# Three closing projections and the products behind them by halves of tokens, with three more pairs of split weights

## What is computed

```python
def rms_norm(x, g):
    y = xf * lax.rsqrt(jnp.mean(xf * xf, axis=-1, keepdims=True) + RMS_EPS)
    return (y * g.astype(jnp.float32)).astype(x.dtype)
...
    x = x + rms_norm(m, mix_post_g[layer])        # m = attention @ w_o
    f = conv_glu_ffn(rms_norm(x, ffn_pre_g[layer]), ...)
    x = x + rms_norm(f, ffn_post_g[layer])        # then kv, q of layer 1, or w_in of block two
```

## Time and profile before

| what | value |
|---|---|
| median of 3 runs | 1725.2 us (1720.46 to 1725.62) |
| the profiled execution, own time | 1720.62 us |
| its span, first to last instruction | 1718.8 us |
| PE busy | 1626.2 us (95%) |
| DVE, ACT, POOL busy | 1026.1, 697.8, 283.5 us |
| mean granted clock of PE | 0.97 |

### The profile page before, as it was taken

The page is one execution under the profiler, slowest core; times in us unless marked ns, Lnnn a source line. Parts: engine busy times, 40 slices in busy tenths (PEclk is TensorE's granted clock), DMA queues, the critical chain, the costliest instruction groups (busy, mean ns, idle before and its releaser), DMA issues.

```text
span 1718.8 us, 20823 instructions
## 1 busy us (share of the span) xinstructions
PE 1626.2 (95%) x7828; PEld 1297.6 (75%) x7828; DVE 1026.1 (60%) x1824; ACT 697.8 (41%) x1349; POOL 283.5 (16%) x227
## 2 busy tenths in 40 slices
PE   6899999999898889999999989999998999999996
PEld 6678888888676668888888867866665788888875
DVE  4766666643767657666663267576666445554364
ACT  4344444332436635444442243244344343333252
POOL 2411111000402213111110035000010021110031
PEclk9899999999898989999999989999999999999998
DMA  4133333323121113333333224221110233333221
GB/s 143 37 99 97 95 98 98 104 93 101 56 68 32 38 55 92 98 97 95 97 99 98 92 62 123 68 56 38 38 44 19 86 86 98 98 98 97 95 92 61
DMA packets 89340, 139.24 MB, mean 81 GB/s; under 512 B 8596, under 2 KB 28564, under 8 KB 89240
## 3 DMA queue, kind: packets, MB, share of 16 engines
q1 hardware_dynamic: 86464, 133.56, 26.4%
q10 hardware_dynamic: 2776, 4.35, 0.8%
HBM read 135.78 MB, written 2.10 MB: 80 GB/s over the span
## 4 chain that ended last, share of the span: by engine, by line
PE 90%; DVE 6%; issue 1%; ACT 1%; POOL 1%; DMA 0%; SPq 0%; POOLq 0%; DVEq 0%; ACTq 0%
PE ps L347 24%; PE ps L349 24%; PE ps L348 24%; PE ps L1580 2%; PE ps L1582 2%; PE ps L1581 2%; PE ps L359 1%; PE ps L1263 1%; PE ps L1286 1%; PE ps L1306 1%; PE ps L381 1%; PE ps L645 1%; PE ps L960 1%; DVE M L485 0%; DVE M L468 0%
## 5 line engine op out<-in xcount | busy, mean ns | idle before, releaser
L335 DVE TENSOR_TENSOR wl<-raw,wh 128x512 fp32r<-128x512 f32 (+2 forms) x472 | 360.9, 767 | 491.8 <-ACT wh L324 491.6
L324 ACT ACTIVATE wh<-raw 128x512 fp32r<-128x512 f32 (+2 forms) x472 | 295.3, 627 | 665.5 <-PE ps L349 658.2
L347 PE MATMUL ps<-Hh,wh 128*128 128x512 f32 (+1 forms) x1336 | 531.9, 398 | 29.0 <-DVE Hl L408 21.0
L349 PE MATMUL ps<-Hh,wl 128*128 128x512 f32 (+1 forms) x1336 | 525.2, 393 | 0.0
L348 PE MATMUL ps<-Hl,wh 128*128 128x512 f32 (+1 forms) x1336 | 525.1, 393 | 0.0
L347 PEld LDWEIGHTS ps<-Hh,wh 128*128 128x128 f32 (+1 forms) x1336 | 253.6, 190 | 95.9 <-DVE Hl L408 28.1
L349 PEld LDWEIGHTS ps<-Hh,wl 128*128 128x128 f32 (+1 forms) x1336 | 253.4, 190 | 54.5 <-issue 0.2
L348 PEld LDWEIGHTS ps<-Hl,wh 128*128 128x128 f32 (+1 forms) x1336 | 253.9, 190 | 52.6 <-issue 0.9
L347 PE MATMUL ps<-AH,wh 128*128 128x512 f32 x480 | 187.1, 390 | 0.0
L349 PE MATMUL ps<-AH,wl 128*128 128x512 f32 x480 | 186.9, 389 | 0.0
L348 PE MATMUL ps<-AL,wh 128*128 128x512 f32 x480 | 186.8, 389 | 0.0
(11 more groups left out here) (254 smaller groups left out, 1653.5 us busy)
## 6 DMA issues: line engine op xcount, KB each, us to landing
raw<-in_w_in SPq DMA_DIRECT2D x216, 256.0 KB, 2.7
raw<-in_w_out SPq DMA_DIRECT2D x104, 256.0 KB, 2.6
raw<-in_w_up SPq DMA_DIRECT2D x64, 256.0 KB, 2.7
raw<-in_w_down SPq DMA_DIRECT2D x32, 256.0 KB, 2.8
raw<-in_w_q SPq DMA_DIRECT2D x16, 256.0 KB, 2.6
raw<-in_w_o SPq DMA_DIRECT2D x16, 256.0 KB, 2.6
raw<-in_w_pg SPq DMA_DIRECT2D x16, 256.0 KB, 2.8
X<-in_xT SPq DMA_DIRECT2D x8, 256.0 KB, 6.0
```

The costliest lines, as they stand in the source:

```text
L324: e.activation(spls[n % NSPL][0][:, 0:width], raws[n % NRAW][:, 0:width], ACT.Copy, scale=1.0 if gain is None else gain).then_inc(s_hi, 1)
L335: e.tensor_tensor(wl[:, 0:width], raw, wh[:, 0:width].bitcast(F32), ALU.subtract).then_inc(s_lo, 1)
L347: e.matmul(b, wh[:, o:o + w], xh, start=k == 0, stop=False)
L349: m = e.matmul(b, wl[:, o:o + w], xh, start=False, stop=k == nk - 1)
```

## The change

At the three boundaries the last three pieces of the closing projection are held back and multiplied for tokens 0 to 255 in all four tiles, then for tokens 256 to 511. The norm of each half is its own chain (`half_*` functions with two blocks of tokens), with a bank of PSUM for each half, and squares are no longer paired: PE sums each half tile by itself. The gain goes into the take, so that the scale is a plain multiplication. The first three right-hand tiles and products of the next stage are done by halves too; POOL now adds tiles 2 (two halves), 4, 5, 6, 7 and DVE 0, 1 (two halves) and 3. Pieces 1 to 3 of the next stage get pairs of their own (`more`, in the arena that the closing projection has partly finished with), so they can be split before the held pieces are free. Three small constants move to make room. `kv`, `in1` and `z` are the stages behind.

```diff
+        more = [(sub(f"xh{i}", [P, NPIECE], 24576 + 4096 * i, F32R), sub(f"xl{i}", [P, NPIECE], 26624 + 4096 * i, F32R))
+                for i in range(3)]
...
-            for n in range(start, start + nk - 1):
+            held = 3 if closing else 1
+            for n in range(start, start + nk - held):
...
-        ON_DVE = (0, 1, 5)
-        ON_POOL = (2, 3, 4, 6, 7)
+        X_ON_DVE = {1: [(0, 1), (1, 1), (5, 1)]}
+        X_ON_POOL = {1: [(2, 1), (3, 1), (4, 1), (6, 1), (7, 1)]}
+        for v in (2, 3, 4):
+            X_ON_DVE[v] = [(0, 0), (1, 0), (0, 1), (1, 1), (3, 1)]
+            X_ON_POOL[v] = [(2, 0), (2, 1), (4, 1), (5, 1), (6, 1), (7, 1)]
...
         def act_rhs(e, j, k):
+            if j in (1, 2, 3):
+                if k == 0:
+                    for half in range(2):
+                        for c in range(3):
+                            rhs_high(e, j, c, half)
+                    rhs_square(e, j, 0)
+                elif k < 6:
+                    rhs_high(e, j, k + 2)
+                    rhs_square(e, j, k)
+                else:
+                    rhs_square(e, j, k)
+                return
...
         def pe_first_group(e, j, name, nk, outs, free):
+            halved = 3 if j in (1, 2, 3) else 0
+            for half in range(2):
+                for k in range(halved):
+                    e.wait_ge(s_hl, rhs_at(f, k, half))
...
+                        m = multiply_half(e, b, wh[:, o:o + w], wl[:, o:o + w], Hh[:, k, :], Hl[:, k, :], half,
+                                          k == 0 and half == 0, False)
...
+                    if k == 0 and half == 0:
+                        half_spread(e, j, 1)
+            for k in range(halved, nk):
...
+        def pe_close(e, q, name, xh, xl, nk):
+            n = first[name] + 2 * nk - 3
+            for half in range(2):
+                for i in range(4):
+                    bank = Q_BANKS[q][i]
+                    if half:
+                        e.wait_ge(s_pev, tile_at(q, 4 + i, 0))
+                    for k in range(3):
+                        if half == 0 and i == 0:
+                            e.wait_ge(s_lo, n + k + 1)
+                        h, l = (x[:, i * P:(i + 1) * P] for x in split_in[n + k])
+                        m = multiply_half(e, bank, h, l, xh[:, nk - 3 + k, :], xl[:, nk - 3 + k, :], half, False, k == 2)
+                        if k == 2:
+                            m.then_inc(s_acc, 1)
+                        if k == 1 and half + i > 0:
+                            a, b = (half, i - 1) if i else (0, 3)
+                            e.wait_ge(s_psq, tile_at(q, 4 + b, a))
+                            half_square(e, q, a, T[POST_T[q][4 + b]], False, b == 3)
+                        if k == 1 and half and i == 3:
+                            half_spread(e, q, 0)
+            e.wait_ge(s_psq, tile_at(q, 7, 1))
+            half_square(e, q, 1, T[POST_T[q][7]], False, True)
+
+        def dve_close(e, q):
+            for i in range(4):
+                half_take(e, q, i, 0)
+            half_variance(e, q, 0)
+            half_take(e, q, 0, 1)
+            half_take(e, q, 1, 1)
+            half_diagonal(e, q, 0)
+            half_take(e, q, 2, 1)
...
         def dve_new_rhs(e, q, j, k):
+            if k == 0 and q > 0:
+                scale_m(e, q, 0, 0)
+                add_m_dve(e, q, 0, 0)
+                half_take(e, q, 3, 1)
+                half_variance(e, q, 1)
+                rhs_low(e, j, 0, 0)
+                scale_m(e, q, 1, 0)
+                add_m_dve(e, q, 1, 0)
+                half_diagonal(e, q, 1)
+                scale_m(e, q, 2, 0)
+                rhs_low(e, j, 1, 0)
+                scale_m(e, q, 0, 1)
+                add_m_dve(e, q, 0, 1)
+                rhs_low(e, j, 2, 0)
+                scale_m(e, q, 1, 1)
+                add_m_dve(e, q, 1, 1)
+                rhs_low(e, j, 0, 1)
+                scale_m(e, q, 2, 1)
+                rhs_low(e, j, 1, 1)
+                scale_m(e, q, 3)
+                add_m_dve(e, q, 3)
+                rhs_low(e, j, 2, 1)
+                scale_m(e, q, 4)
+            elif q > 0:
+                if k < 4:
+                    scale_m(e, q, k + 4)
+                if k < 6:
+                    rhs_low(e, j, k + 2)
```

More of the change, by code:

```diff
@@ L251, in build, with group @@
         n_acc = n_used = 0
-        def group(name, g, start, nk, tiles):
+        def group(name, g, start, nk, tiles, closing=False):
             nonlocal n_acc, n_used
             acc_base[name, g] = n_acc
-            for n in range(start, start + nk - 1):
+            held = 3 if closing else 1
+            for n in range(start, start + nk - held):
                 n_used += 1
                 used[n] = (s_used, n_used)
-            n_acc += tiles
-            used[start + nk - 1] = (s_acc, n_acc)
+            n_acc += tiles * (2 if closing else 1)
+            for n in range(start + nk - held, start + nk):
+                used[n] = (s_acc, n_acc)
         for n in (0, 2):
@@ L269, in build @@
             for g in range(2):
-                group("out" + name, g, first["out" + name] + NTILE[l] * g, NTILE[l], 4)
+                group("out" + name, g, first["out" + name] + NTILE[l] * g, NTILE[l], 4, l < 2 and g == 1)
             if l == 0:
@@ L384, in keep_root, with half_bank, half_square @@
         def keep_root(e, k, bank):
-            e.wait_ge(s_spread, k)
+            e.wait_ge(s_spread, CHAIN_AT[k] - 1)
             e.activation(RB[:, :], bank[:, :], ACT.Copy).then_inc(s_rb, 1)
+        def half_bank(q, half):
+            return Q_BANKS[q][POST_BANK + half]
+        def half_square(e, q, half, sq, begin, end):
+            bank, o = half_bank(q, half), 256 * half
+            for b in range(2):
+                m = e.matmul(bank[:, o + b:o + b + 1], sq[:, (2 * half + b) * P:(2 * half + b + 1) * P], mean[:, 0:1],
+                             start=begin and b == 0, stop=True, skip_group_check=True)
+            if end:
+                m.then_inc(s_stat, 1)
@@ new lines, in act_close, with half_take @@
+        def act_close(e, q, name):
+            for half in range(2):
+                for i in range(4):
+                    e.wait_ge(s_acc, acc_base[name, 1] + 4 * half + i + 1)
+                    if half == 0 and i == 0:
+                        e.wait_ge(s_pair, pairs_at(q) + 2)
+                    c = slice(256 * half, 256 * half + 256)
+                    e.activation(T[POST_T[q][4 + i]][:, c], Q_BANKS[q][i][:, c], ACT.Square).then_inc(s_psq, 1)
+        def half_take(e, q, i, half):
+            e.wait_ge(s_psq, tile_at(q, 4 + i, half))
+            c = slice(256 * half, 256 * half + 256)
+            e.tensor_scalar(M[:, 4 + i, c], Q_BANKS[q][i][:, c], col(POST_GAIN[q], 4 + i), None,
+                            ALU.mult).then_inc(s_pev, 1)
@@ L742, in pe_ffn @@
                 outs = [L_BANKS[l][4 * ((G + h) % 2) + i][:, :] for i in range(4)]
-                for k in range(nt):
+                closing = l < 2 and h == 1
+                for k in range(nt - 3 if closing else nt):
                     if h == 0:
@@ L811, in dve_ffn @@
                         dve_rotation(e, k)
+                if l < 2 and h == 1:
+                    dve_close(e, q + 1)
+                    continue
                 for i in range(4):
@@ L836, in gpsimd_ffn @@
             if l < 2:
-                root(e, POST_CHAIN[q])
+                for half in range(2 if q else 0):
+                    half_root(e, q, half)
+                if q == 0:
+                    root(e, POST_CHAIN[0])
                 add_m_pool(e, q)
```

270 lines of the change are left out of this document (176 added, 94 removed).

## The result

| | before | after |
|---|---|---|
| median of six runs | 1725.2 us | 1731.5 us |
| range of the runs | 1720.5 to 1726.6 | 1728.6 to 1733.5 |
| ratio, 95% interval | | 1.0043 [1.0027, 1.0059] |
| the profiled execution | 1720.6 us | 1733.5 us |

The change makes the kernel 6.3 us slower, where 8 were forecast. This is one comparison; further down the same kernel comes out 4.5 us apart in two of them, so the sign is firm and the size is not. The two profiled executions are 12.9 us apart, since before's is one of its fastest and after's is its slowest.

The account below looks back on a forecast made before the run. PE, busy 1626.2 of 1718.8 us, was taken as the bound, gated by POOL's sums. Boundaries of +2.1, +2.3 and +3.4 made about +8: span about 1727, 1733 against the 1725.2 median; range 1711 to 1740.

Parts of the forecast that it names:

- main case: At three boundaries PE waits for POOL's later sums and the clock falls: +8 us, 1733 against the median; chance 0.42.
- How well the gate was hidden: Behind product 6 PE needs POOL's six sums of squares, today hidden by only 0.9, 0.3 and 1.2 us.
- DVE's list: From first spread to last scale DVE needs 17.1 us instead of 11.8; POOL's last addition ends 19 us after that spread.
- short waits for the second spread and ACT, +1.3: Part of DVE's added time between the first spread and the end of its last scale: 1.3 us per boundary.
- rival (d): Low clock also catches the half products opening the new stage, at most one boundary: +5 us, 1738; chance 0.05.
- The six sums: POOL's six sums at 1.71 us each, 10.25 in all as today, ending at 461.7 instead of 460.4 at the first boundary.
- (b): POOL's six sums meet few collisions, 2.7 us less each boundary, and the clock stays up: 1716 us; chance 0.15.
- (c): POOL's sums are ready when PE asks, so product 7 starts 5.2 us sooner or more: 1707 us; chance 0.11.
- The low clock behind the gate: After 6.9 us of only mean squares, product 7 starts at 1.2 GHz: +2.0 us at the first boundary.
- Rival (a): Clock holds through the light stretch or sums end a microsecond sooner: about 1726 us; chance 0.27 shared with late halves.
- The third boundary: ACT's five transfers delay the first right-hand half, starting 2 us later than in the second stage: boundary +3.4 us.
- Rival (e): Halves wait for the whole root, starting behind the second spread near 437; same time as the clock holding, shared chance 0.27.

Follow-up runs that it names:

- e5_warm: Changed kernel plus four fp32 products of 512 columns, unused in the result, in PE's wait between the two mean squares: 1725.9 us, ratio 1.000 to before.
- moderate: Changed kernel with four POOL sums, scale 5, one split, then scales 6 and 7, constants' transfers later: 1714.7 and 1719.2 us, 0.994 and 0.9966 of before.
- with filler: The moderate kernel plus one unused fp32 product of 512 columns behind each closing's last half square: 1718.9 and 1718.3 us, 0.997 and 0.996 of before.
- all in full: Changed kernel with four POOL sums, scales 4 to 7 in a row ahead of the splits, constants' transfers later: 1728.4 and 1729.9 us, both 1.002 of before.

## Why the prediction was right, and where its terms were off

- **The main case held:** 1733 forecast, 1731.5 measured. The mechanism is the one forecast, a gate that was hidden and is not any more. Its three signs are all there: first products 5.2 us sooner at the first boundary (5.9 forecast), a new wait for the sums of 4.0 us three times (4 to 5), the clock at 0.50 when product 7 starts.
- **How well the gate was hidden was misread:** the prediction has PE ask for the sums at the start of its two mean squares (461.36). The last sum is needed by the second of them, some 0.8 us later, so the sums were hidden by 1.8, 1.2 and 2.0 us, not 0.9, 0.3 and 1.2. The forecast does not suffer, since it uses only the differences between the three, and in the new order it rightly does one mean square ahead of the wait.
- **DVE's list:** POOL's last addition was to end 19 us after the first spread; it ended 21.5, 20.4 and 23.4 after. The step was right, its size short by 1 to 4 us. The term that was mis-sized is "short waits for the second spread and ACT, +1.3": DVE idles 1.97 us for the second spread alone at the first boundary. In part it was made good by luck: the first spread came 12.3 and 11.6 us behind the start of the closing at the first two boundaries, where 12.9 were forecast.
- **The reason is rival (d), in part.** It was given 0.05 as a case of its own, since "PE's gaps there are under 1 us". They were 1.09 and 2.73 us, and the clock fell at the first and third boundary (in 436 to 440, and from 1017). Twelve half products then took 12 x 0.21 instead of 12 x 0.12, 1.1 us, and the second spread came that much later: 2.6 us behind the first new product, against 1.5 at the second boundary, where the clock fell only behind it (638.04). This accounts for most of the +4.0 instead of +2.1 at the first boundary, with +2.2 of it ahead of product 7; the second, which escaped it, gave +1.6, less than forecast. The kernel with filler products (e5_warm) allows a comparison here, since it is the same up to the first mean square and its clock held in this hole:

```profile
435.37 0.39 PE L412 MATMUL ps<-Hh,wh 128*128 128x256 f32 x1 [1.09 <-DVE Hl L514]
436.92 0.59 PE L482 MATMUL ps<-DG,ones 128*128 128x256 f32 x2
...
452.14 10.16 POOL L529 TENSOR_TENSOR M<-M 128x512 f32<-128x512 f32 x6
```

Both kernels reach the first new product 15.5 us behind the start of the closing (419.89 here). From there the second spread comes 1.6 us behind it, not 2.6, and the sums end 42.4 us behind the start of the closing, not 43.9. The forecast was 42.2. So this fall costs 1.5 us at the first boundary. Why the clock held in one execution and fell in the other, behind the same idle 1.09 us, is open.
- **The six sums:** 10.15, 10.14 and 10.06 us, where the earlier trace rows were taken over unchanged. Right, and rivals (b) and (c) fell with it.
- **The low clock behind the gate:** +2.0 forecast per boundary. From product 7 to the second group it took 6.4, 5.8 and 7.1 us against 4.6 before, so 1.9, 1.3 and 2.6. Rival (a) fell; the kernel with filler products confirms the size.
- **The third boundary:** the first right-hand half was to start 2 us later than in the second. It starts 2.69 us after the start of the last square (1014.99 to 1017.68), in the second 0.63 (634.79 to 635.42): 2.1 later. With the fall of the clock on top it cost +5.8, not +3.4.

```profile
634.79 0.39 ACT L655 ACTIVATE t<-ps 128x256 f32<-128x256 f32 x1 [1.58 <-PE ps L414]
635.42 0.51 ACT L507 ACTIVATE Hh<-X,cols 128x256 fp32r<-128x256 f32 x1 [0.24 <-DVE X L686]
...
1014.99 0.39 ACT L655 ACTIVATE t<-ps 128x256 f32<-128x256 f32 x1 [1.59 <-PE ps L414]
...
1017.13 0.45 ACTq L1964 DMA_DIRECT2D b_w<-in_cmp_w  x1
1017.68 0.51 ACT L507 ACTIVATE Hh<-X,cols 128x256 fp32r<-128x256 f32 x1 [2.30 <-issue]
```

- **Rival (e)** fell: the first half products start 2.6, 1.5 and 2.7 us ahead of the second spread.
- The sum was made against a profiled execution of 1720.6 us and gave about 1729 for it; the new profile is 1733.5. The 4 us missed there and the 4.6 by which the old profile lay under its own median nearly cancel. That is luck: the forecast of 1733 was nearer than its terms.

What a version without the three new pairs of split weights would do was not tried.

## What to carry to other kernels

Before you shorten a hole, list what the engine must pass next and by how much that is hidden today: here it was POOL's sums, hidden by 1.2 to 2.0 us, and they cost 23 us where the halves had won 17. When one engine's list feeds both the bottleneck and a helper that gates it, the order in that list is the change. The order of the scales alone and fewer sums alone each came to about 1720 us, and both to the full, with the transfers later, only to 1728 and 1730: remedies do not add up. Run a version more than once before you believe a difference of 4 us.

## What the runs showed of the hardware

**The clock also falls where nothing was changed, and the same kernel does it again.** Summing (1 - granted clock) over the span gives the time lost to the low clock, if PE always has work. Taken outside the three boundaries, it can be set beside the length of the boundaries and the time of the profiled execution (us):

| kernel | profiled run | three boundaries | lost outside them | what is left |
|---|---|---|---|---|
| before | 1720.6 | 144.5 | 31.3 | 1544.8 |
| after | 1733.5 | 155.8 | 33.2 | 1544.5 |
| scales in a row | 1713.6 | 142.7 | 22.5 | 1548.4 |
| moderate, two runs | 1716.0; 1719.2 | 140.9; 143.3 | 30.7; 29.0 | 1544.4; 1546.9 |
| with filler, two runs | 1719.3; 1718.3 | 138.7; 138.7 | 33.2; 33.1 | 1547.4; 1546.5 |
| all in full, two runs | 1732.7; 1730.1 | 148.1; 148.0 | 40.9; 38.3 | 1543.7; 1543.8 |

What is left agrees within 5 us over kernels that lie 20 us apart. So two terms make most of the difference, and one of them is in no part of the code that was edited. The losses come in portions of 1.7 us; the +1.5, -1.6 and +1.7 us between before and after outside the boundaries are one portion more, one less and one more (+1.7, -1.7 and +1.9 us lost there). The windows of the first and the second run of the full version, and last those of the second run of the moderate one, at the same places of the stage behind the third boundary:

```profile
1106.00:1107.00 1.00, 1.00 (x4) 0.81 (x3) 0.55 (x1) 0.39 (x1) 0.00 (x0) 0.50 0.00 0
1197.00:1198.00 1.00, 1.00 (x4) 0.81 (x3) 0.92 (x7) 0.00 (x0) 0.00 (x0) 0.50 0.00 0
```

```profile
1106.00:1107.00 1.00, 1.00 (x4) 0.81 (x3) 0.00 (x0) 0.00 (x0) 0.00 (x0) 0.50 0.15 17
1196.00:1197.00 1.00, 1.00 (x4) 0.76 (x3) 0.93 (x7) 0.00 (x0) 0.00 (x0) 0.50 0.00 0
```

```profile
1100.00:1101.00 1.00, 1.00 (x8) 0.61 (x6) 0.15 (x1) 0.20 (x1) 0.00 (x0) 1.00 0.00 0
1191.00:1192.00 1.00, 1.00 (x5) 0.32 (x3) 0.29 (x1) 0.60 (x1) 0.00 (x0) 1.00 0.27 24
```

Both runs of the full version lose the clock at the same places, and the moderate one, whose third boundary ends some 6 us sooner, keeps it there. Between 1060 and 1700 us the full version loses eight and seven portions, the moderate one three in both of its runs. An earlier end is not the reason: the two runs with the filler end that boundary sooner still (1038.8 and 1037.8) and lose seven. Their stretch behind it is 5.9 us longer than in the moderate version (678.8 against 672.9) with 5.9 us more lost (19.5 against 13.6), and this takes back what their boundaries had won.

The repeats on other chips show that these falls mostly come back with a kernel. They do not always: of the twelve executions of the second run of the full version, two took 1721.1 and 1721.5 us at a mean granted clock of 0.979, the others 1725.7 to 1732.7 at 0.970 to 0.976. What decides them stays open.

**What one turn costs.** The six sums beside DVE's splits take 10.15 / 6 = 1.69 us each in the changed kernel (1.71 before); four of them, with the scales in a row, 6.82 / 4 = 1.71.

**What PE did before the clock fell, and where it held.** Eight one-column passes and a wait of 4 us brought it to 0.50; eight passes of 512 columns in the same wait kept it up. It also fell without any wait: behind the 24 one-column passes in a row of the moderate version (2.9 us) at two of three boundaries in one run and at all three in the other. Behind the 16 of the kernel before (1.84 us) it fell at none.
